# Forming two of the four weight sums of each seven-product feed-forward panel by accumulating DMAs from GpSimd

## What is computed

```
def swiglu(h, w_gate_up, w_down):
    gate, up = jnp.split(h @ w_gate_up, 2, axis=-1)
    return (jax.nn.silu(gate) * up) @ w_down

x = x + swiglu(rms_norm(x, ffn_norm[layer]), ffn_w_gate_up[layer], ffn_w_down[layer])
```

## Time and profile before

| | |
|---|---|
| median of three runs | 2197.89 us |
| the profiled execution, its own time | 2200.72 us |
| its span, first to last instruction | 2197.3 us |
| TensorE busy (matmul) | 2115.2 us, 96% |
| VectorE busy | 1467.1 us, 67% |
| ScalarE busy | 933.6 us, 42% |
| GpSimd busy | 53.4 us, 2% |
| DMA engines, share of the span (queue q1) | 20.3% |
| mean granted TensorE clock | 0.975 of full speed |

### The profile page before, as it was taken

The page is one execution under the profiler, slowest core; times in us unless marked ns, Lnnn a source line. Parts: engine busy times, 40 slices in busy tenths (PEclk is TensorE's granted clock), DMA queues, the critical chain, the costliest instruction groups (busy, mean ns, idle before and its releaser), DMA issues. The chain is left out here.

```text
span 2197.3 us, 37822 instructions
## 1 busy us (share of the span) xinstructions
PE 2115.2 (96%) x15297; PEld 1827.9 (83%) x15297; DVE 1467.1 (67%) x2882; ACT 933.6 (42%) x1806; POOL 53.4 (2%) x33
## 2 busy tenths in 40 slices
PE   8998999899999999989999999999999999899997
PEld 8996667799988977879998887887888788678885
DVE  5257875888755777598886455656656665665567
ACT  5246872555400467345550015433433343355444
POOL 1110000000000300000000000000000000000000
PEclk9999999999999999999999999999999999889998
DMA  4230001232332320113233212112111110212211
GB/s 181 97 112 19 1 1 62 83 116 97 106 115 84 106 72 20 58 68 116 97 106 115 96 67 78 43 55 76 41 54 57 59 55 0 94 39 97 77 40 39
DMA packets 30666, 159.37 MB, mean 73 GB/s; under 512 B 3392, under 2 KB 3904, under 8 KB 17856
## 3 DMA queue, kind: packets, MB, share of 16 engines
q1 hardware_dynamic: 30240, 157.24, 20.3%
q10 hardware_dynamic: 288, 0.20, 0.0%
HBM read 155.33 MB, written 2.10 MB: 72 GB/s over the span
## 5 line engine op out<-in xcount | busy, mean ns | idle before, releaser
L224 PE MATMUL ps<-late_parts,panel_upper 128*128 128x256 f32 (+1 forms) x1392 | 468.0, 336 | 0.0
L223 PE MATMUL ps<-late_parts,panel_upper 128*128 128x512 f32 (+1 forms) x1276 | 441.9, 346 | 10.1 <-DVE arena_sb L1658 7.2
L225 PE MATMUL ps<-late_parts,panel_parts 128*128 128x512 f32 (+1 forms) x1276 | 433.3, 340 | 0.0
L219 DVE TENSOR_TENSOR panel_parts<-panel_sb,panel_upper 128x512 fp32r<-128x512 f32 (+1 forms) x344 | 348.6, 1042 | 17.6 <-ACT panel_upper L723 8.4
L223 PE MATMUL ps<-panel_upper,hT_parts 128*128 128x256 f32 (+2 forms) x964 | 300.2, 311 | 7.5 <-DVE h_lower L911 7.5
L225 PE MATMUL ps<-panel_upper,h_lower 128*128 128x256 f32 (+2 forms) x964 | 286.8, 298 | 0.0
L224 PEld LDWEIGHTS ps<-late_parts,panel_upper 128*128 128x128 f32 x1392 | 264.7, 190 | 26.4 <-issue 0.2
L224 PE MATMUL ps<-panel_parts,hT_parts 128*128 128x256 f32 (+2 forms) x964 | 285.8, 297 | 0.0
L223 PEld LDWEIGHTS ps<-late_parts,panel_upper 128*128 128x128 f32 x1276 | 242.8, 190 | 41.7 <-DVE arena_sb L1658 7.4
L225 PEld LDWEIGHTS ps<-late_parts,panel_parts 128*128 128x128 f32 x1276 | 243.7, 191 | 29.6
L223 PE MATMUL ps<-hT_parts,panel_upper 128*128 128x512 f32 (+1 forms) x508 | 203.7, 401 | 4.2 <-DVE h_lower L3260 2.5
(11 more groups left out here) (512 smaller groups left out, 3714.1 us busy)
## 6 DMA issues: line engine op xcount, KB each, us to landing
panel_sb<-ffn_gate_up_w SPq DMA_DIRECT2D x76, 512.0 KB, 4.4
panel_sb<-gdn_w SPq DMA_DIRECT2D x24, 1024.0 KB, 4.9
panel_sb<-ffn_down_w SPq DMA_DIRECT2D x22, 1024.0 KB, 4.9
panel_sb<-nsa_w SPq DMA_DIRECT2D x13, 1024.0 KB, 5.0
panel_sb<-gla_w SPq DMA_DIRECT2D x12, 1024.0 KB, 4.8
panel_sb<-gdn_out_w SPq DMA_DIRECT2D x8, 1024.0 KB, 4.8
panel_sb<-ffn_gate_up_w SPq DMA_DIRECT2D x6, 1024.0 KB, 4.8
panel_sb<-nsa_out_w SPq DMA_DIRECT2D x4, 1024.0 KB, 4.8
```

Of the source, the lines that this page charges most:

```text
L219: return engine.tensor_tensor(out, src, hi.bitcast(F32), ALU.subtract)
L223: mm(out, w_hi, x_hi, start=start, stop=False, skip_group_check=skip_group_check)
L224: mm(out, w_hi, x_lo, start=False, stop=False, skip_group_check=skip_group_check)
L225: return mm(out, w_lo, x_hi, start=False, stop=stop, skip_group_check=skip_group_check)
```

## The change

s1 and s3 are no longer added on VectorE. SyncE issues a third DMA per panel, which loads m21 a second time, from HBM into the place of s1 (256 KB). It goes out after the bottom half of the same panel and waits for `fifth` of two panels before. Then GpSimd issues two DMAs per panel that read a block from HBM and add it to what lies in SBUF: m11 onto m21 (this gives s3), after the bottom half has landed; and m22 onto the copy of m21 (this gives s1), after the copy has landed. ScalarE waits for both before it makes the high part of s1 or s3, and VectorE waits for both before it adds s2. The copy of m21 counts on the same semaphore as the top half, so whoever waits for the top half (m11, m12) waits for the copy as well. `nth(b)` is b - 2, and is above 2 from panel 5 on.

```
-    SUM_ORDER = ("s1", "s3", "s2", "s4")
+    SUM_ORDER = ("s2", "s4")
...
+    FFN_DONE.update({f"dma_sums{n}": 32 * sum(b % 2 == n for b in range(PLAIN_PANELS, FC)) for n in range(2)})
+    FFN_DONE.update({f"top{n}": 32 * sum(b % 3 == n for b in range(PLAIN_PANELS, FC)) for n in range(3)})
...
             sp.dma_start(whole[:, 2 * BLOCK_COLS:], src[b, :, 2 * BLOCK_COLS:]).then_inc(landed[slot], 16)
+            if nth(b) > 2:
+                sp.wait_ge(S("ffn_product"), after(f, "product", PRODUCT_AT["p5", b - 2]))
+            else:
+                sp.wait_ge(used[SUMS_SLOT], sp_panels.done[SUMS_SLOT] + 1)
+            sp.dma_start(weights(f, "s1", b)[0], src[b, :, 2 * BLOCK_COLS:3 * BLOCK_COLS]).then_inc(S(f"ffn_top{b % 3}"), 16)
...
+    def summed_by_dma(eng, f, b):
+        eng.wait_ge(S(f"ffn_dma_sums{b % 2}"), after(f, f"dma_sums{b % 2}", 32 * ((b - PLAIN_PANELS) // 2 + 1)))
+
+    def pool_ffn(pool, f):
+        src = io[f"{f}_gate_up_w"]
+        for b in range(PLAIN_PANELS, FC):
+            bottom_landed(pool, pool_panels, f, b)
+            if nth(b) > 2:
+                pool.wait_ge(S("ffn_low"), after(f, "low", LOW_AT["s3", b - 2]))
+            pool.dma_start(weights(f, "s3", b)[0], src[b, :, 0:BLOCK_COLS], accum_op=ALU.add).then_inc(S(f"ffn_dma_sums{b % 2}"), 16)
+            top_landed(pool, f, b)
+            pool.dma_start(weights(f, "s1", b)[0], src[b, :, 3 * BLOCK_COLS:], accum_op=ALU.add).then_inc(S(f"ffn_dma_sums{b % 2}"), 16)
+        ffn_passed(f, pool_panels)
...
-        eng.wait_ge(S(f"ffn_top{b % 3}"), after(f, f"top{b % 3}", (b // 3) * 16))
+        eng.wait_ge(S(f"ffn_top{b % 3}"), after(f, f"top{b % 3}", (b // 3) * 32))
...
+                elif name in ("s1", "s3"):
+                    summed_by_dma(act, f, b)
...
             for name in names:
-                if name == "s1":
+                if name == "s2":
                     top_landed(dve, f, b)
-                    bottom_landed(dve, dve_panels, f, b)
...
-                        dve.wait_ge(S("ffn_product"), after(f, "product", PRODUCT_AT["p5", b - 2]))
-                    last = nc.vector.tensor_tensor(plain["s1"], m21, plain["m22"], ALU.add)
-                elif name == "s3":
-                    last = nc.vector.tensor_tensor(plain["s3"], m21, plain["m11"], ALU.add)
...
+                    summed_by_dma(dve, f, b)
                     last = nc.vector.tensor_tensor(plain["s2"], plain["s1"], plain["m11"], ALU.add)
...
-        add_w(b, "s1", "s3")
...
-        add_w(b + 1, "s1", "s3")
...
-                add_w(b + 2, "s1", "s3", "s2")
+                add_w(b + 2, "s2")
...
             pool_nsa(pool)
+            nsa_passed(pool_panels)
+            pool_ffn(pool, "ffn0")
             pool_mla(pool)
+            mla_passed(pool_panels)
+            pool_ffn(pool, "ffn1")
```

More of the change, by code:

```diff
@@ L188, in build_in @@
     split = [nc.alloc_semaphore(f"panel{s}_split") for s in range(SLOTS)]
-    sp_panels, pe_panels, pe_splits, act_panels, dve_panels = [Panels() for _ in range(5)]
+    sp_panels, pe_panels, pe_splits, act_panels, dve_panels, pool_panels = [Panels() for _ in range(6)]
     def load_panel(sp, slot, src, tiles, i=0):
@@ L1298, in build_in @@
                 "high": (FC - PLAIN_PANELS) * len(HIGH_ORDER), "low": len(LOW_AT), "product": len(PRODUCT_AT), "moved_out": len(OUT_AT), "combined": len(COMBINED_AT)}
-    FFN_DONE.update({f"top{n}": 16 * sum(b % 3 == n for b in range(PLAIN_PANELS, FC)) for n in range(3)})
+    FFN_DONE.update({f"dma_sums{n}": 32 * sum(b % 2 == n for b in range(PLAIN_PANELS, FC)) for n in range(2)})
+    FFN_DONE.update({f"top{n}": 32 * sum(b % 3 == n for b in range(PLAIN_PANELS, FC)) for n in range(3)})
     def after(f, name, n):
@@ L1624, in add_w @@
             plain = {name: weights(f, name, b)[0] for name in HIGH_ORDER}
-            m21 = plain["s3"]
             for name in names:
-                if name == "s1":
+                if name == "s2":
                     top_landed(dve, f, b)
-                    bottom_landed(dve, dve_panels, f, b)
                     if b == PLAIN_PANELS:
@@ L1632, in add_w @@
                     if nth(b) > 2:
-                        dve.wait_ge(S("ffn_product"), after(f, "product", PRODUCT_AT["p5", b - 2]))
-                    last = nc.vector.tensor_tensor(plain["s1"], m21, plain["m22"], ALU.add)
-                elif name == "s3":
-                    last = nc.vector.tensor_tensor(plain["s3"], m21, plain["m11"], ALU.add)
-                elif name == "s2":
-                    if nth(b) > 2:
                         dve.wait_ge(S("ffn_product"), after(f, "product", PRODUCT_AT["p6", b - 2]))
-                    dve.wait_ge(S("ffn_sum"), after(f, "sum", summed("s1", b)))
+                    summed_by_dma(dve, f, b)
                     last = nc.vector.tensor_tensor(plain["s2"], plain["s1"], plain["m11"], ALU.add)
```

## The result

The changed kernel takes 2361.97 us, the median of four runs (2355.89 to 2363.74), against 2198.32 us for the kernel before, measured with them. The ratio is 1.0738 (95% interval 1.0718 to 1.0759): slower by 164 us. The forecast was slower, 2259 us, with a range of 2212 to 2325. The direction was right, and so was the cycle that the prediction built; the size was not, by 103 us, and the time lies 37 us above the range.

The account below looks back on a forecast made before the run. TensorE was taken to bound the loop, VectorE's sums hidden; waiting for the DMA sums makes 32 steps 2.06 us longer, +66, less 4.8 before the loops: +61 us, 2259 us, range 2212 to 2325.

Parts of the forecast that it names:

- the cycle: FFN loop, load to next load: A + 6.98 us, hidden below 9.92; forecast as a step of 11.98 us.
- A: FFN loop, from the bottom half's landing until VectorE knows both sums: 5.0 us taken, hidden up to 2.94.
- The gain before the loop: Before each FFN loop, four sums fewer ahead of `c11(3)` on VectorE: 2.4 us per FFN, -4.8 us in all.
- The copy of m21 and ScalarE's first casts: FFN panels: SyncE's extra 256 KB load and the casts about 3 us later were both taken to cost nothing.
- slow sums: Rival, FFN loop: DMA sums much slower than a load, A above 6.6; at 7.4, 2336 us; chance 0.10.
- The clock: Rival: TensorE's clock falls to 0.50 at each stop; 1.1 us more a step if only `fourth`, 2295 us; chance 0.10.
- the attention stretch: Sign against the clock's fall: there TensorE is busy only 8.21 of 10 us and keeps its full clock.
- The fast-sums rival: FFN loop: A at or below 2.94 us, nothing stalls and only the start gains, 2193 us; chance 0.12.

Follow-up runs that it names:

- filler: The changed kernel with 24 matmuls, their result never read, in front of each `fourth` of panels 4 to 19: 2332.05 us.
- start_only: DMA sums for panels 3, 4 and 5 of each FFN alone, panels 6 to 21 as in the kernel before: 2193.06 us.
- own_sem: The changed kernel with the copy of m21 counted on its own semaphore and one semaphore for both DMA sums: 2364.12 us.
- late_top: The changed kernel, but SyncE issues the next panel's top half only after both sums of this panel have landed: 2351.86 us.
- plain_pool: The changed kernel with GpSimd's two DMAs loading instead of adding, that part of the computation left out: 2289.2 us.
- plain_sp: The changed kernel with two plain loads in place of the DMA sums, issued by SyncE behind the next top half: 2273.4 us.
- s3_only: The changed kernel with only s3 formed by an accumulating DMA, s1 back on VectorE and no copy of m21: 2211.1 us.
- c22_first: The changed kernel with the waits for DMA sums moved behind `c22` on VectorE and later on ScalarE, m21's copy counted apart: 2225.82 us.

## Why the prediction was right or wrong

*What bounds the kernel, and the cycle: right.* The prediction said that a step would last from the landing over A, s2 and `c22` to the end of `fourth`. With the filler's clock, nearly always full in `fourth`, that chain gives 14.04 us, and 14.27 is measured. In the changed kernel the 32 waits for `c22`, VectorE idle in front of s2 and ScalarE's later casts are all there.

*The gain before the loop: right.* -4.8 us was forecast, -4.8 measured in start_only. The wait for `c11(3)` is 5.2 us where 5.1 was forecast.

*The copy of m21 and ScalarE's first casts at nothing: right.* own_sem shows the second. The copy delays the second sum now and then: GpSimd waited for it 12 times, 10.4 us in all, 0.3 us a step. In late_top this wait is nearly gone (2.4 us in all), and the two sums take as long as before.

*A: the step that failed.* The prediction took s2 to start 3.97 + 5.0 = 8.97 us after the bottom load. It starts at 11.04, 2.07 later. Of this 0.54 us is the front: GpSimd starts the first sum at 4.51, where VectorE had started its own at 3.97. The rest is A, 11.04 - 4.51 = 6.53 us in place of 5.0. The mis-sized term is the landing of the two sums, 512 KB taken "like one bottom load, which takes 4.1 us to land", to which one issue of 0.9 was added. GpSimd's second issue begins 1.05 us after the first (5.56 - 4.51), not far from that. But this second DMA (line 1359) then lands 5.3 us after its issue, at the median, and not 4.1:

```profile
DMA to landing us min/median/max: 4.8/5.3/6.3
```

What made it long is the adding. Without it (plain_pool) the same stretch takes 4.89 us, which is the prediction's 5.0; with it 6.53. Issuing from SyncE takes s2 a further 0.5 us forward (plain_sp). That "each transfer also reads what it adds to" stood in the prediction, but only as a ground for the size of an issue; in plain_pool's figures the two sums need 1.56 us more of the DMA engines, and A would have been 6.6. Counted as the prediction did, from 3.97, A is 11.04 - 3.97 = 7.07 us: past the 6.6 at which its rival "slow sums" (0.10) began, and by the first of the causes that this rival named.

*The clock: a rival at 0.10 that came true.* The prediction let the attention stretch, with 8.21 of 10 us busy at full clock, speak against it. There, from 205 to 330 us, the idle time came in pieces of at most 1.4 us; here it came in one piece of 3.2 us on average. Its price was worked out as 1.1 us a step, 36 us; filler gives 0.88 and 30.

The step of the change is 3.17 us above the forecast's 11.98: 2.07 in the start of s2, 0.88 in the clock, and about 0.2 in the way from the end of `c22` to the next load, which took 1.65 us in the prediction and 1.84 in filler. 32 x 3.17 = 101 us on 2259 makes 2360, and 2361.97 is measured.

Neither of the two would have left the range by itself: s2 at 11.04 makes 2325 us, just its upper end, and the clock alone was priced at 2295. The range had room for the milder half of one or the other, and the two came together. The prediction had no case for both, although the longer A is, the longer TensorE stands idle.

*The fast-sums rival* needed s2 by 6.9 us. Even plain loads from SyncE let it start only at 8.83. The estimate from the Trainium skill ("DMA: Bandwidth & Descriptors", Anatomy of one DMA), 2.0 us plus bytes over 436 GB/s, gave 2.6 us for 256 KB. The traces don't agree: an accumulating DMA of 256 KB from GpSimd, with no second one from GpSimd beside it (s3_only), lands at 4.1 us at the least and 4.2 at the median from its issue, 0.86 of it being the issue; a plain one in plain_pool at 3.2 and 3.6, with 0.54 for the issue.

What stays open: why the first sum starts 0.54 us later than VectorE's did. The bottom loads of the change land at a median of 4.3 us after issue, where they took 4.1 before, which is 0.2 of it. From SyncE (plain_sp) the first of the two loads starts 0.3 us earlier than from GpSimd (4.14 and 4.45), but there the bottom half lands 0.2 us earlier too; GpSimd's reaction to the semaphore was not taken apart. Two orders were not tried: summing s1 before s3, so that s2 waits for the first of them only, and loading the copy of m21 before the bottom half.

## What to carry to other kernels

Work taken off an engine that isn't the bound gains nothing, and the DMA that takes its place adds a latency; what counts is what is queued behind the wait for it. Close the cycle (load, landing, sum, the waiting instruction, the product that frees the buffer) before the change: here there were 2.9 us to spare for a thing that takes 6.5. The same DMAs cost 28 us instead of 164 where the wait stood behind the urgent work (c22_first), and gained 4.8 where the data came 20 us ahead (start_only).

When a new stall is forecast on TensorE, price the clock with it, and price it in the same case as the stall: here stalls of 3.2 us in steps of 15 went with the lower level in most steps and made 30 of the 164 us.

## What the runs showed of the hardware

- An accumulating DMA from HBM onto SBUF in float32 occupied the DMA engines 1.62 us for 256 KB, a plain one 0.84: about 127 to 136 GB/s at 0.76 to 0.89 of full use (the change, 506 to 510 us), against 268 at 0.90 for plain loads from SyncE (before).
- GpSimd needed 0.86 us to issue an accumulating DMA of 256 KB and 0.54 us for a plain one; SyncE mostly 0.33 to 0.43.
- Two accumulating DMAs, one after the other, took 6.5 us from the start of the first to the add that waits for both, whether the second started 1.05 us behind the first (the change) or 0.65 (late_top).
- More matmuls made the kernel faster: 24 useless ones in each stalled step raised the mean granted clock from 0.947 to 0.976 and saved 30 us.
